# The first mixer of a three-layer block: the next pair's projections placed between the products of the inverse

## The reference, cut to what matters

```python
mod = c_act @ ada_w[layer] + ada_b[layer]        # 1024 -> 6144, shifts, scales and gates
h = rmsnorm(x, g) * (1.0 + scale_m) + shift_m
proj = h @ w_in                                  # q, k, v, gate: 4 x 1024; decay and beta: 2 x 8
qkv = silu(causal_depthwise_conv(qkv, conv_w))   # 4 taps
q = l2norm(q) * 128 ** -0.5;  k = l2norm(k)
# for each head and chunk: A = I + strict_lower((beta k) k^T * decay)
u = triangular_solve(A, v * beta);  w = triangular_solve(A, beta * k * exp(g_cum))
# over the chunks: v_new = u - w S;  o = q_dec S + attn v_new;  S = S * exp(g_last) + k_dec^T v_new
x = x + gate_m * ((rmsnorm(o) * silu(gate)) @ w_out)
```

## Time and profile before

| | us |
|---|---|
| median of 3 runs (2761.06 to 2765.28) | 2762.79 |
| the profiled execution's own time | 2765.61 |
| its span | 2763.8 |
| PE busy | 2512.9 |
| DVE busy | 1189.4 |
| ACT busy | 921.1 |
| POOL busy | 379.4 |

### The profile page before, as it was taken

How to read it: one execution, slowest core, us unless ns; L and a number is a source line. 1 busy time by engine, 2 the same in 40 slices (tenths; PEclk the granted TensorE clock), 3 DMA queues, 4 the chain that set the end, 5 groups by cost and what they waited for, 6 DMA issues and landing times.

```text
span 2763.8 us, 29796 instructions
## 1 busy us (share of the span) xinstructions
PE 2512.9 (91%) x11632; PEld 1992.0 (72%) x11632; DVE 1189.4 (43%) x1192; ACT 921.1 (33%) x1043; POOL 379.4 (14%) x164
## 2 busy tenths in 40 slices
PE   8689898978999998888999999999997788999997
PEld 7477777766888886555788887678775567788886
DVE  1565564735543235554433324443226533433224
ACT  2244352543332123433333123433324432333222
POOL 0264756531441000000000000000000000000000
PEclk6799999999999999789999999999998899999999
DMA  5122322212333232322222222211220022222222
GB/s 216 61 99 115 121 76 106 92 75 92 122 142 117 91 107 76 106 81 76 78 100 91 91 92 103 91 70 61 78 90 31 16 75 76 82 101 91 92 91 91
DMA packets 34909, 253.12 MB, mean 92 GB/s; under 512 B 3872, under 2 KB 4128, under 8 KB 4640
## 3 DMA queue, kind: packets, MB, share of 16 engines
q1 hardware_dynamic: 34848, 252.25, 25.3%
HBM read 250.13 MB, written 2.10 MB: 91 GB/s over the span
## 4 chain that ended last, share of the span: by engine, by line
PE 83%; DVE 8%; issue 4%; ACT 4%; DMA 1%; DVEq 0%; ACTq 0%; SPq 0%
PE D L255 19%; PE D L256 19%; PE D L257 19%; PE D L270 3%; PE D L271 2%; PE D L272 2%; PE D L870 2%; PE D L342 2%; PE D L879 2%; PE D L1098 1%; DVE lo L303 1%; PE D L1097 1%; DVE xi L781 1%; PE D L291 1%; PE D L292 1%
## 5 line engine op out<-in xcount | busy, mean ns | idle before, releaser
L255 PE MATMUL D<-hH,lo 128*128 128x512 f32 x1712 | 693.6, 405 | 0.3 <-DVE lo L303 0.3
L256 PE MATMUL D<-hL,hi 128*128 128x512 f32 x1712 | 677.5, 396 | 0.0
L257 PE MATMUL D<-hH,hi 128*128 128x512 f32 x1712 | 677.1, 396 | 0.0
L303 DVE TENSOR_TENSOR lo<-raw,hi 128x2048 fp32r<-128x2048 f32 (+1 forms) x185 | 451.6, 2441 | 422.9 <-ACT hi L299 422.9
L299 ACT ACTIVATE hi<-raw 128x2048 fp32r<-128x2048 f32 (+1 forms) x185 | 342.9, 1854 | 495.3 <-PE D L257 292.0
L255 PEld LDWEIGHTS D<-hH,lo 128*128 128x128 f32 x1712 | 323.8, 189 | 91.6 <-issue 17.6
L256 PEld LDWEIGHTS D<-hL,hi 128*128 128x128 f32 x1712 | 323.7, 189 | 80.5 <-issue 6.9
L257 PEld LDWEIGHTS D<-hH,hi 128*128 128x128 f32 x1712 | 323.2, 189 | 76.8
L312 POOL TENSOR_TENSOR adar<-adar 128x1024 f32<-128x1024 f32 (+2 forms) x120 | 228.9, 1907 | 9.4
L310 POOL TENSOR_TENSOR adar<-adar,cact 128x2048 f32<-128x2048 f32 x40 | 150.3, 3758 | 462.1 <-DMA adar<-in_ada 462.1
L255 PE MATMUL D<-aH,lo 128*128 128x512 f32 x444 | 176.0, 396 | 0.0
(11 more groups left out here) (366 smaller groups left out, 3319.8 us busy)
## 6 DMA issues: line engine op xcount, KB each, us to landing
raw<-in_slabs SPq DMA_DIRECT2D x185, 1024.0 KB, 4.8
adar<-in_ada SPq DMA_DIRECT2D x44, 1024.0 KB, 4.9
go<-in_ada SPq DMA_DIRECT2D x4, 1024.0 KB, 10.4
x<-in_xin SPq DMA_DIRECT2D x1, 2048.0 KB, 10.0
out<-x SPq DMA_DIRECT2D x1, 2048.0 KB, 6.3
tab<-in_rope SPq DMA_DIRECT2D x1, 1792.0 KB, 7.3
vb<-in_vbias SPq DMA_DIRECT2D x1, 576.0 KB, 8.7
lvl<-in_masks SPq DMA_DIRECT2D x1, 448.0 KB, 7.6
```

The source lines that it names most:

```text
L255: T_.matmul(o, lo[s.slot][:, w], H[:, k, :], start=(k == 0), stop=False)
L256: T_.matmul(o, hi[s.slot][:, w], L[:, k, :], start=False, stop=False)
L257: last = T_.matmul(o, hi[s.slot][:, w], H[:, k, :], start=False, stop=(k == kc - 1))
L303: V_.tensor_tensor(lo[s.slot][:, 0:n], raw[s.slot][:, 0:n], hi[s.slot][:, 0:n], ALU.subtract).then_inc(lo_ready, 1)
```

## The change

1. *Pipeline.* The loops over pairs are written out. While PE works on the inverse and the state of pair p, it also takes 48 steps of projections for pair p+1, through a generator (`product_steps`, `fill(n)`): in front pairs four steps a level, all between the level's first and second products, and the others around the head of the chain and in the state loop. Four slabs (q, k, v of pair 0, q of pair 1) are taken ahead of pair 0. The gate slabs come last: gate 0 in pair 2, gates 1 to 3 in pair 3 (three steps between the products and three after).
2. *Halves.* Projections use D[1] alone, one bank for each head, freed by `half_free` and `bank_free`; the level's second product and the transpose share D[2]; D[3][:, 0] (`W`) takes sums of squares and the transposes of k and v. Convolution, silu and norms go head by head, between the levels.
3. *Rows.* They are written to DRAM and read back by SP, spread over 128 partitions (`rows_out`, `row_in`), in place of the `along` matmuls. The rows chain is cut in pieces between the first projections.
4. *Output.* The output norm and gate are applied later, within the next pair; in the last pair `to_h` runs beside the state loop.
5. *First conditioning.* The 8 blocks are multiplied with `cact` as a 32-column weight (`cpad`, one column used), 256 columns of `ada_w` moving, into four 32-partition strips of a bank, which a matmul with ones then sums (`first_rows_pe`, `first_cols_pe`). Their first two loads are issued ahead of `x`.
6. *Conditioning blocks.* Six in each pair in place of eight, and one for each of 16 feed-forward slabs in place of one for two. POOL starts on them after `tsc` is there.

The diff, cut to its core:

```diff
-ADA_P = 8
+ADA_P = 6
...
+        def first_rows_pe(pe, g, h):
...
+            for r in range(2):
+                for q in range(4):
+                    k = 4 * r + q
+                    last = T_.matmul(row_bank[h][32 * q:32 * q + 32, :], cpad[:, k, :], w3[:, 2 * k * P:2 * (k + 1) * P],
+                                     start=(r == 0), stop=(r == 1))
...
+        W = D[3][:, 0, :]
+        unit_bank = lambda s, m: D[0 if s == K_SEQ(0) else 1][:, m, :]
...
@@ gdn_act @@
+                def level(lv):
                     for m in range(2):
+                        pb_copy(lv, m)
+                        if lv > 1:
+                            zz_copy(lv - 1, m)
...
@@ gdn_dve @@
+                split_lo(dve, Slab(6 + 3 * p))
+                level(2)
+                if front:
+                    conv(ks, 1, x, K_SEQ(x), 0)
...
+                v_turned(0)
+                level(3)
+                v_turned(1)
...
+                level(4)
+                if front:
+                    conv(ks, 1, x, K_SEQ(x), 1)
...
+                split_lo(dve, Slab(7 + 3 * p))
+                level(5)
+                level(6)
+                if front:
+                    q_norm(x)
+                    conv(vs, 2, x, V_SEQ(x), 0)
...
+                state(2)
+                split_lo(dve, Slab(8 + 3 * p))
+                if front:
+                    beta_decay(x)
+                    k_norm(x)
+                if p < 2:
+                    conv(qs[p % 2], 0, p + 2, Q_SEQ(p + 2), 0)
...
@@ gdn_pe @@
+            fill(32)
+            rows_pe(pe)
+            fill(8)
+            w("tsc", 1)
+            sum_squares(fs, 0, 1)
...
+                lv_fill = (4, 0) if front else (3, 3)
...
+                for b in range(2 * NT):
+                    last = T_.matmul(blk(D[2], b), blk(ks, b), blk(qp, b), start=True, stop=True)
+                last.then_inc(gg["qk"], 1)
+                fill(3)
+                for m in range(2):
+                    w("xx", 14 * p + m + 1)
+                    turn(0, m, D[0])
...
                 for lv in range(1, 7):
                     for m in range(2):
...
+                        if lv > 1:
+                            turn(lv - 1, m, D[2])
...
+                    fill(lv_fill[0])
                     for m in range(2):
+                        w("pb", 12 * p + 2 * (lv - 1) + m + 1)
...
+                    fill(lv_fill[1])
...
                 for t in range(NT):
...
+                    fill(2 if front or t < 2 else 0)
...
+                    if front:
+                        fill(2)
+                    elif t < 2:
+                        fill(2 - t)
...
@@ the block of SP @@
+            rows_out(sp)
+            row_in(sp, dt, 0, 0, "gc_in")
...
-            both(G_FFN0 + 1, ada1, left // 2, 4, (0, 1, 0, 1))
+            both(G_FFN0 + 1, ada1, left // 4, 4, (1, 1, 1, 1))
```

More of the change, by code:

```diff
@@ new lines, in first_cols_pe, with first_act @@
+        def first_cols_pe(pe, g, h):
+            pe.wait_ge(row_ready, 2 * g + h + 1)
+            for m in range(2):
+                last = T_.matmul(first_bank[g][:, 2 * h + m:2 * h + m + 1], st[:, 2 * h + m, :], ones[:, 0:1],
+                                 start=True, stop=True)
+            last.then_inc(first_col, 1)
+        def first_act(act, g):
+            for h in range(2):
+                row_summed(act, g, h)
+                S_.activation(st[:, 2 * h:2 * h + 2, :].rearrange("p a n -> p (a n)"), row_bank[h],
+                              ACT.Copy).then_inc(row_ready, 1)
@@ L607, in rows_dve, with rows_dve_4 @@
                              ALU.subtract).then_inc(gg["rowd"], 1)
+        def rows_dve_4(dve):
+            beta, nbe, w_ = rows[:, 1, :], rows[:, 3, :], rtmp[:, 2, :]
             dve.wait_ge(gg["row"], 5)
@@ L610, in rows_dve, with tsc_dve @@
                                     op1=ALU.mult).then_inc(gg["rowd"], 1)
+        def tsc_dve(dve):
             dve.wait_ge(gg["rowp"], 1)
[L612 to L622, removed]
-            S_.activation(gc, gc, ACT.Ln).then_inc(gg["row"], 1)
-            act.wait_ge(gg["rowd"], 2)
-            S_.activation(w_, gc, ACT.Exp).then_inc(gg["row"], 1)
-            S_.activation(dl, u_, ACT.Exp).then_inc(gg["row"], 1)
+            V_.tensor_copy(tsc[:].rearrange("p a t h -> p (a t h)"), W[:, 0:4 * NT * GH]).then_inc(gg["tsc"], 1)
+            dve.wait_ge(gg["tsc"], 1)
         def rows_pe(pe):
@@ L887, in body @@
+                    if lv in (1, 3, 5):
+                        ada_at(lv // 2)
+                    fill(lv_fill[1])
+                for m in range(2):
+                    w("xx", 14 * p + 13 + m)
+                    turn(6, m, D[2])
+                fill(1 if front else 0)
+                w("zz", 12 * p + 12)
+                w("kd", 2 * p + 2)
                 for b in range(2 * NT):
-                    last = T_.matmul(blk(D[0], b), blk(kb, b), blk(zi, b), start=True, stop=True)
+                    last = T_.matmul(blk(D[2], b), blk(kbT, b), blk(zi, b), start=True, stop=True)
```

865 lines of the change are left out of this document (573 added, 292 removed).

## The result

| | us |
|---|---|
| changed kernel, median of 4 runs (2634.73 to 2641.05) | 2636.1 |
| kernel before, in the same comparison | 2764.0 |
| difference | -127.9 |
| ratio | 0.954, 95% interval 0.9523 to 0.9557 |
| predicted | 2656, range 2616 to 2700 |

The account below looks back on a forecast made before the run. It took the alternation of PE with DVE and ACT, with projections and chain run serially, as the bound: 61 + 62 + 3 x 98 + 92 = 509 against 618.0, +2 after, net -107, giving 2656 us, range 2616 to 2700.

Parts of the forecast that it names:

- fast rival: Whole mixer: all waits covered and conditioning strips parallel, pairs of 88 us, a saving of 154 to 2609; chance 0.12.
- issue sum of a pair: Front pair: all PE instructions added up, 86 us, taken as the lower bound with every wait covered.
- 12 us of waits in a pair: Front pair: PE waiting at six kinds of place, together 9 to 16 us, taken as 12, giving a 98 us pair.
- T0: First stage: end of the decay and beta product, forecast at 61 us against 84.5 before, with ends 53 and 85.
- rival with a first stage that gains nothing: Conditioning: PE stays at half clock and strips run one after another, product ends at 85 us, kernel 2680; chance 0.15.
- To the first blocks: Stretch from the decay and beta product's end to the first k k^T blocks: 62 us forecast, 87.0 before.
- (c): Within a pair: v's transpose waits for the scaled first half, behind a convolution, 1 to 2 us.
- (d): State loop: `vn` of t = 2 waits for ACT's norm logarithm and exponential, 1 us a pair.
- (e): Within a pair: the output norm must come before W is free, 1 us of waiting.
- (a): Around the chain's head: DVE work up to the first masked copy, 15 to 22 us, leaves PE waiting 3 to 5.
- (b): Ahead of level 2's masked copies: DVE's scalings, products and a split, 7 to 11 us, come 0 to 4 late.
- (f): Across a pair: some twenty changes between steps and small blocks, each with a handoff of 0.1 to 0.2, 3 us.

Follow-up runs that it names:

- one-strip run: Changed kernel with all eight wide conditioning matmuls of a block summed into one 32-partition PSUM strip instead of four in turn: 2650.0 us, ratio 0.9592.
- added-work runs: Changed kernel with seven added small VectorE instructions in each front pair, ahead of level 2's masked copies (2644.1 us) or level 4's (2659.5 us).

## Why the prediction was right, point by point

The forecast, 2656 us, is 20 us above what was measured, and the fast rival, 2609, is 27 below; at the output product's first matmul (485.5 us) the forecast (509) and that rival (462) are equally far off. The cover of the round trips and the issue sum of a pair were right. The step that failed is the 12 us of waits in a pair: by the prediction's own last sentence its account of the pair is wrong if the pair comes down to 88, and pairs 0 and 1 took 88.2 us. Their mean with pair 2, 89.1, is also outside the 90 to 108 that the range was built from. That the time lies in the range all the same is because the range goes further down than three pairs of 90 would take it, which would be 24 of its 40 us.

- *T0.* 61 forecast, 58.3 measured, partly by luck, since two errors offset. The mis-sized term is the group of conditioning, 6.9 us for 1.9: the last group waits for its block until 36.5 us and ends at 38.4, where my sum had it near 46. But from there to the product's first matmul it is 5.9 us and not 2, as PE waits 4.05 us for DVE's split of the slab. With groups of 7 us, my own price, the one-strip run ends the product at 69.6 us. The rival with a first stage that gains nothing is out. PE in order of time in the changed kernel:

```profile
36.51 1.94 PE L352 MATMUL D<-go,dt 128*32 128x256 f32 x16 [1.41 <-DMA go<-in_ada]
...
44.30 0.80 PE L275 MATMUL D<-hH,lo 128*128 128x512 f32 x1 [4.05 <-DVE lo L308]
```

- *To the first blocks.* 62 for 65.9. PE's wait for the rows was 7.6 us (8 forecast), and they came 29.9 us after T0 (31 forecast). The mis-sized term is what follows, 36.0 us for 31. Part of it is DVE behind POOL: the instructions for decay and q's norm there took 2.4, 4.5 and 3.4 us for 1.3, 1.2 and 1.5 in pair 1; the run with POOL cut has the whole stretch at 59.6 us. PE also waits 3.5 us there for the norm of k, which the sum had hidden beside the steps. Two rows of DVE from this stretch, with POOL at work from 94.7 to 115.6 us:

```profile
105.84 4.51 DVE L920 TENSOR_TENSOR dt<-dt,cst 128x1024 f32<-128x1024 f32 x1
110.27 3.37 DVE L933 SCALAR_TENSOR_TENSOR qs<-qs,fs 128x1024 f32<-128x1024 f32 x1
```

- *The pair.* 98 for 89.1 on average, the step that missed. The issue sum was right (86 for 85.4; half of 1.98 is 0.99 and not the 0.9 that it has for a matmul with ones, which would add 0.5). The waits were 12 in the sum and 2.8 in pair 1: (c) 1.6 came as written, (d) 0.7 and (e) 0.3 came a little smaller, and (a) 3 to 5, (b) 0 to 4 and (f), the 3 us of handoffs, left nothing; the last 0.2 us are for a masked copy of level 6. (a) and (b) were priced with the split's mean of 4.47 us, that is, I took contention as a property of the instruction, when it belongs to the place. That DVE had 0.65 us to spare at (b) shows how near it was: with a split of 4.47 us there in place of 2.29, PE would have waited some 1.5 us in that place (an estimate from these rows). Pair 2, with gate 0, has 2.6 us more: the logarithm of the output norm (L888) stands behind the gate's silu on ScalarE, and PE waits 2.8 us for it.
- *Last pair.* 92 for 94.1. PE waits 7.9 us in it, and 3.65 of them for POOL at a conditioning sum, a price that I had set at nothing; 2.1 are for ScalarE's silu of a gate. The granted clock is 0.94. With POOL cut the pair took 87.6 us. PE in order of time:

```profile
481.87 1.01 PE L414 MATMUL D<-cst,adar 128*128 128x1 f32 x4 [3.65 <-POOL adar L317]
```

- *After.* +2 for +1.7, which says nothing, since that stretch varies by 7 us from profile to profile.
- *Rivals.* Round trips not hidden: out, PE waits 0.2 us for masked copies. DVE's queue as the path: out at this load, but the added-work runs show its mechanism at its place. The fast rival had the pairs (88) and the strips side by side right, and T0 too (57 for 58.3); it missed the first blocks (58 for 65.9) and the last pair (83 for 94.1).

What stays open: why the handoffs cost so little, why shifting POOL by one level met no split, and why the unchanged code behind the mixer takes up to 7 us more in some profiles (its mean clock is 0.95 there, and 0.96 in the changed kernel's).

## What to carry to other kernels

Independent matmuls placed between the dependent steps of a chain are worth their full time if the round trip over the other engines is shorter than they are, and the count of PE instructions then gives nearly the time (85.4 of 88.2 us here); where exactly they stand is settled by the slowest trip, and should be tried on both sides. Read the slack of each place of an in-order queue from the idle time ahead of the instruction that the chain needs, not from the engine's total. A wait of PE can cost more than its length, by the clock that falls behind it (6.1 us of waiting, 8.1 us of pair). And put VectorE work with two SBUF inputs where GpSimd is idle; work that reads PSUM can stand beside it (the convolution's first instruction kept its 0.745 us).

## What the runs showed of the hardware that I had not expected

Matmuls with 32-column weights, spread over four strips in turn, started every 0.06 us, and the same ones into one strip every 0.22, with the same 0.379 us of length in the records; the gain shows only in the spacing. And a 384-column VectorE instruction of 0.56 us took 1.77 us on average beside GpSimd instructions of 1.6 to 4 us.
